# Causal attention without its empty quarter, with a fused score and row extremum

## The reference

```python
s_o = jnp.einsum('bhqd,bhkd->bhqk', qc, ko).astype(jnp.float32) * scale
s_o = s_o + table_h[:, t5_bucket(rel_o)]
s_o = jnp.where(rel_o >= 0, s_o, -jnp.inf)
...
p = jax.nn.softmax(logits, axis=-1)
```

```python
s = jnp.where(mb, s, NEG_INF)
m = jnp.maximum(jnp.max(s, axis=-1, keepdims=True), sink)
p = jnp.exp(s - m)
denom = jnp.sum(p, axis=-1, keepdims=True) + jnp.exp(sink - m)
return jnp.einsum('bkgqs,bskd->bqkgd', (p / denom).astype(vbb.dtype), vbb)
```

## Time and profile before

| | us |
|---|---|
| median of 3 timed runs | 3369.41 (3365.79 to 3370.77) |
| profiled execution, span from first to last instruction | 3367.9 |
| PE busy in it | 3090.6 (92%) |
| DVE busy | 2435.7 (72%) |
| ACT busy | 1680.4 (50%) |
| POOL busy | 134.1 (4%) |
| mean granted TensorE clock | 0.931 of full |

### The profile page before, as it was taken

How to read it: one execution, slowest core, us unless ns; L and a number is a source line. 1 busy time by engine, 2 the same in 40 slices (tenths; PEclk the granted TensorE clock), 3 DMA queues, 4 the chain that set the end, 5 groups by cost and what they waited for, 6 DMA issues and landing times. The chain is left out here.

```text
span 3367.9 us, 58567 instructions
## 1 busy us (share of the span) xinstructions
PE 3090.6 (92%) x23849; PEld 2753.4 (82%) x23849; DVE 2435.7 (72%) x3648; ACT 1680.4 (50%) x2444; POOL 134.1 (4%) x152
## 2 busy tenths in 40 slices
PE   7679999899888899999987999999899998988899
PEld 6577777689887789898976899899689898978798
DVE  6669999778765468787577587785668788674555
ACT  4437777654552354544553445544554545442444
POOL 0010000100102000000000000000000000011000
PEclk8779999999999799999986999999899999998899
DMA  9347999767410267586430386774057687300442
GB/s 383 141 175 295 370 369 366 292 244 307 188 69 4 78 253 307 225 312 262 162 128 1 119 312 262 265 307 193 11 225 306 231 310 272 123 2 3 160 183 83
DMA packets 77517, 698.67 MB, mean 207 GB/s; under 512 B 8432, under 2 KB 12528, under 8 KB 55408
## 3 DMA queue, kind: packets, MB, share of 16 engines
q1 hardware_dynamic: 30928, 525.65, 39.7%
q10 hardware_dynamic: 42912, 157.31, 12.3%
q0 software_dynamic: 3456, 12.58, 1.0%
HBM read 691.31 MB, written 4.19 MB: 207 GB/s over the span
## 5 line engine op out<-in xcount | busy, mean ns | idle before, releaser
L1074 PE MATMUL banks<-u_split,w_split 128*128 128x512 f32 x2816 | 1014.9, 403 | 22.9 <-DVE u_split L1319 21.0
L1143 ACT ACTIVATE w_split<-ring 128x1024 fp32r<-128x1024 f32 x513 | 541.3, 1058 | 672.1 <-PE banks L1075 406.5
L1250 DVE TENSOR_TENSOR w_split<-ring,w_split 128x1024 fp32r<-128x1024 f32 x513 | 625.5, 1222 | 293.3 <-ACT w_split L1143 288.7
L1075 PE MATMUL banks<-u_split,w_split 128*128 128x256 f32 x2816 | 797.3, 283 | 0.0
L1074 PEld LDWEIGHTS banks<-u_split,w_split 128*128 128x128 f32 x2816 | 537.3, 191 | 158.8 <-issue 17.9
L1075 PEld LDWEIGHTS banks<-u_split,w_split 128*128 128x128 f32 x2816 | 539.7, 192 | 0.0
L1066 PE MATMUL banks<-h_split,w_split 128*128 128x256 f32 x1408 | 400.6, 285 | 7.9 <-DVE w_split L1250 7.9
L1067 PE MATMUL banks<-h_split,w_split 128*128 128x256 f32 x1408 | 400.5, 284 | 0.0
L1068 PE MATMUL banks<-h_split,w_split 128*128 128x256 f32 x1408 | 400.4, 284 | 0.0
L520 PE MATMUL banks<-bufs_split,ring_split 128*128 128x256 f32 x1376 | 397.0, 289 | 0.0
L584 DVE CUSTOM_DVE_ANT_0 bufs<-bufs 128x1024 f32<-128x1024 f32 x300 | 357.0, 1224 | 12.7 <-DVE w_split L1250 12.7
(11 more groups left out here) (489 smaller groups left out, 4931.5 us busy)
## 6 DMA issues: line engine op xcount, KB each, us to landing
ring<-stream SPq DMA_DIRECT2D x155, 3072.0 KB, 10.9
bufs<-ada ACTq DMA_DIRECT2D x296, 512.0 KB, 10.4
bufs<-ada POOLq DMA_DIRECT2D x23, 512.0 KB, 6.7
bufs<-ada SPq DMA_DIRECT2D x3, 2048.0 KB, 16.1
ring<-stream SPq DMA_DIRECT2D x2, 2688.0 KB, 10.0
bufs<-c_rows SPq DMA_DIRECT2D x9, 512.0 KB, 4.3
ring<-stream SPq DMA_DIRECT2D x1, 2704.0 KB, 13.1
ring<-stream SPq DMA_DIRECT2D x1, 2176.0 KB, 8.9
```

Of the source, the lines that this page charges most:

```text
L1074: pe.matmul(bank.rearrange("p (a t) -> p a t", a=2), w_high, u_split[:, k, :, :], start=(k == 0), stop=False, skip_group_check=True)
L1075: return pe.matmul(bank[:, 0:SEQ], w_low, u_split[:, k, 0, :], start=False, stop=(k == KC - 1), skip_group_check=True)
L1143: nc.scalar.activation(w_split[:, slot, 0, :], piece(j, b), ACT.Copy).then_inc(high.sem, 1)
L1250: e = nc.vector.tensor_tensor(w_split[:, slot, 1, :], piece(j, b), w_split[:, slot, 0, :].bitcast(F32), ALU.subtract)
```

## The change

The row of a head now holds 384 columns instead of 512: 128 keys for the first query tile, 256 for the second (`CAUSAL = P + SEQ`). Scores, bias, exponentials, scalings, transposes (three) and the second product with v are cut to it.

DVE's scale, add, maximum and negation become one fused instruction per query tile, which forms minus the scaled score (with a bias that is stored 8 times larger) and keeps the row's minimum, starting from minus the sink. ACT then takes the exponential with scale -1.

The sink becomes a column of the row: POOL writes minus the sink at both ends of the buffer, so the exponential of the row and its sum take it along. The two separate exponentials and the addition on DVE are gone.

```diff
+CAUSAL = P + SEQ
...
-                act.activation(rows[h // 4][:, (h % 4) * 512:(h % 4 + 1) * 512], bank(h), ACT.Copy)\
+                act.activation(rows[h // 4][:, (h % 4) * 512:(h % 4 + 1) * 512], bank(h), ACT.Copy, scale=HEAD ** 0.5)\
...
-                    src = bass.AP(core.scratch.tensor, h * 2 * SEQ + (SEQ - 1) - t * P, [[HEADS_A * 2 * SEQ - 1, P], [1, SEQ]])
-                    sync.dma_start(bias[:, h, t, :], src).then_inc(read.sem, read.count(16))
+                    src = bass.AP(core.scratch.tensor, h * 2 * SEQ + (SEQ - 1) - t * P, [[HEADS_A * 2 * SEQ - 1, P], [1, (t + 1) * P]])
+                    sync.dma_start(bias[:, h, t * P:t * P + (t + 1) * P], src).then_inc(read.sem, read.count(16))
...
+    less_sinks = core.small[:, 96:96 + heads]
+    bank = lambda n, h: core.psum[:, 2 * n + h % 2, :]
+    keys = (slice(0, P), slice(P, CAUSAL))
+    with_sink = (slice(0, P + 1), slice(P + 1, CAUSAL + 2)) if sinks is not None else (slice(1, P + 1), slice(P + 1, CAUSAL + 1))
+    inner = (slice(1, P + 1), slice(P + 1, CAUSAL + 1))
...
+                if sinks is not None:
+                    pool.tensor_scalar(less_sinks, sinks, -1.0, None, ALU.mult).then_inc(sinks_negated.sem, sinks_negated.count(1))
+                    pool.wait_ge(sinks_negated.sem, sinks_negated.at(1))
+                    for h in range(heads):
+                        if h >= 2:
+                            pool.wait_ge(exped.sem, exped.at(h - 1))
+                        pool.tensor_copy(s_buf(h)[:, 0:1], less_sinks[:, h:h + 1])
+                        pool.tensor_copy(s_buf(h)[:, CAUSAL + 1:CAUSAL + 2], less_sinks[:, h:h + 1]).then_inc(sink_placed.sem, sink_placed.count(1))
...
-                    last = pe.matmul(bank(0, h)[:, t, :], q(h)[:, t * P:(t + 1) * P], k(h), start=True, stop=True)
+                    last = pe.matmul(bank(0, h)[:, keys[t]], q(h)[:, t * P:(t + 1) * P], k(h)[:, 0:(t + 1) * P], start=True, stop=True)
...
-                for kt in range(2):
-                    for t in range(2):
-                        last = pe.transpose(bank(1, h)[:, kt, t * P:(t + 1) * P], p_buf(h)[:, t, kt * P:(kt + 1) * P], ident)
+                for part in range(3):
+                    last = pe.transpose(bank(1, h)[:, part * P:(part + 1) * P], p_buf(h)[:, 1 + part * P:1 + (part + 1) * P], ident)
...
+                pe.matmul(rows[:, 0:SEQ], v(h, 0), pt_buf(h)[:, 0:SEQ], start=True, stop=False, skip_group_check=True)
+                pe.matmul(rows[:, P:SEQ], v(h, 1), pt_buf(h)[:, SEQ:CAUSAL], start=False, stop=True, skip_group_check=True)\
...
+            if sinks is not None:
+                dve.wait_ge(sinks_negated.sem, sinks_negated.at(1))
...
-                link(dve.scalar_tensor_tensor(s_buf(h), bank(0, h), scale, bias(h), ALU.mult, ALU.add))
-                link(dve.tensor_reduce(stat(h, 0), s_buf(h), AX, ALU.max))
-                if sinks is None:
-                    last = dve.tensor_scalar(stat(h, 1), stat(h, 0), -1.0, None, ALU.mult)
-                else:
-                    last = dve.tensor_scalar(stat(h, 1), stat(h, 0), sinks[:, h:h + 1], -1.0, ALU.max, ALU.mult)
+                if h >= 2:
+                    dve.wait_ge(exped.sem, exped.at(h - 1))
+                for t in range(2):
+                    last = dve.tensor_tensor_reduce(s_buf(h)[:, inner[t]], bank(0, h)[:, keys[t]], bias(h)[:, keys[t]], -scale,
+                                                    3e38 if sinks is None else less_sinks[:, h:h + 1], ALU.add, ALU.min, stat(h, 0)[:, t:t + 1])
...
+                if sinks is not None:
+                    act.wait_ge(sink_placed.sem, sink_placed.at(h + 1))
...
-                    if sinks is not None:
-                        act.activation(stat(h, 3)[:, t:t + 1], sinks[:, h:h + 1], ACT.Exp, bias=stat(h, 1)[:, t:t + 1])
-                    e = act.activation(p_buf(h)[:, t, :], s_buf(h)[:, t, :], ACT.Exp, bias=stat(h, 1)[:, t:t + 1],
-                                       accum_out=stat(h, 2)[:, t:t + 1])
+                    e = act.activation(p_buf(h)[:, with_sink[t]], s_buf(h)[:, with_sink[t]], ACT.Exp, bias=stat(h, 0)[:, t:t + 1], scale=-1.0,
+                                       accum_out=stat(h, 1)[:, t:t + 1])
```

More of the change, by code:

```diff
@@ L282, in const_plan @@
              ("causal", 2 * P), ("zeros", P), ("slide", 2 * RW_HEADS - 2),
-             ("band", 2 * SEQ), ("buckets", 2 * SEQ)]
+             ("band", CAUSAL), ("buckets", 2 * SEQ)]
     place, at = {}, 0
@@ L316, in const_array @@
     put("causal", np.concatenate([i[:, None] < i[None, :], i[:, None] <= i[None, :]], axis=1).astype(np.float32))
-    band = np.zeros((P, 2, SEQ), np.float32)
+    band = []
     for t in range(2):
-        rel = (t * P + i)[:, None] - np.arange(SEQ)[None, :]
-        band[:, t] = np.where((rel >= 0) & (rel < P), 0.0, NEG)
-    put("band", band.reshape(P, -1))
+        rel = (t * P + i)[:, None] - np.arange((t + 1) * P)[None, :]
+        band.append(np.where((rel >= 0) & (rel < P), 0.0, NEG))
+    put("band", np.concatenate(band, axis=1))
     dist = (SEQ - 1) - np.arange(2 * SEQ)
@@ L1637, in attend @@
                     pe.wait_ge(stored.sem, stored.at(h - 1))
[L1638 to L1642, removed]
+                rows = bank(2, h)[HEAD * (h % 2):HEAD * (h % 2) + HEAD, :]
+                pe.matmul(rows[:, 0:SEQ], v(h, 0), pt_buf(h)[:, 0:SEQ], start=True, stop=False, skip_group_check=True)
+                pe.matmul(rows[:, P:SEQ], v(h, 1), pt_buf(h)[:, SEQ:CAUSAL], start=False, stop=True, skip_group_check=True)\
+                    .then_inc(attended.sem, attended.count(1))
             scores(0)
@@ L1670, in softmax_out @@
                 dve.wait_ge(exped.sem, exped.at(h + 1))
-                if sinks is not None:
[L1672 to L1675, removed]
+                link(dve.reciprocal(stat(h, 2), stat(h, 1)))
+                dve.tensor_scalar(p_buf(h)[:, inner[0]], p_buf(h)[:, inner[0]], stat(h, 2)[:, 0:1], None, ALU.mult)
+                dve.tensor_scalar(p_buf(h)[:, inner[1]], p_buf(h)[:, inner[1]], stat(h, 2)[:, 1:2], None, ALU.mult)\
                     .then_inc(normed.sem, normed.count(1))
@@ L1700, in turned_copy @@
                     act.wait_ge(attended.sem, attended.at(h - 1))
-                act.activation(pt_buf(h), bank(1, h), ACT.Copy).then_inc(turned_sb.sem, turned_sb.count(1))
+                act.activation(pt_buf(h), bank(1, h)[:, 0:CAUSAL], ACT.Copy).then_inc(turned_sb.sem, turned_sb.count(1))
             def head_out(h):
@@ L1705, in head_out @@
                 base = HEAD * (h % 2)
-                act.activation(out(h), bank(2, h)[base:base + HEAD, 0, :], ACT.Copy).then_inc(stored.sem, stored.count(1))
+                act.activation(out(h), bank(2, h)[base:base + HEAD, 0:SEQ], ACT.Copy).then_inc(stored.sem, stored.count(1))
             exps(0)
@@ L2344, in first_block @@
     attention_stage(core, HEADS_A, lambda h: rows(qk[:, 0:4, :], h), lambda h: rows(qk[:, 4:8, :], h),
[L2345 to L2348, removed]
+                    lambda h, kt: v_tok[:, kt, HEAD * h:HEAD * h + HEAD], lambda h: bias[:, h, 0:CAUSAL],
+                    lambda h: rows(attn_out, h), lambda h: core.bufs[:, 6, 512 * (h % 2):512 * (h % 2) + CAUSAL + 2],
+                    lambda h: core.bufs[:, 6, 1024 + 512 * (h % 2):1024 + 512 * (h % 2) + CAUSAL + 2],
+                    lambda h: core.bufs[:, 7, 512 * (h % 2):512 * (h % 2) + CAUSAL], beside=lambda pool: later.load(pool, LATER_SUMS["pair_norm"]))
     pair_norm_stage(core, core.buf(0), core.buf(9), (core.col("norm_lru_g"), core.col("norm_attn_g")), later)
@@ L2407, in _ @@
             core.load_ahead(sync, ("sw_v", 0))
-            core.load_const(sync, "band", core.bufs[:, 7, D:D + 2 * SEQ])
+            core.load_const(sync, "band", core.bufs[:, 7, D:D + CAUSAL])
         @block.tensor
@@ L2501, in window_attention @@
     window_projection_stage(core, u, core.mod[:, 3 * KC:4 * KC], qk, v_tok, core.buf(4, 2), lambda c: core.col("q_norm" if c < 8 else "k_norm"))
-    band = core.bufs[:, 7, D:D + 2 * SEQ].rearrange("p (a t) -> p a t", a=2)
+    band = core.bufs[:, 7, D:D + CAUSAL]
     rows = lambda x, c, h: x[HEAD * (h % 2):HEAD * (h % 2) + HEAD, c, :]
```

16 lines of the change are left out of this document (8 added, 8 removed).

## The result

The changed kernel takes 3378.63 us (median of 9 runs, 3373.69 to 3383.89), the kernel before 3370.77 (9 runs, 3365.25 to 3379.30). The ratio is 1.0025, 95% interval 1.0015 to 1.0035: slower by a quarter of a percent where 0.5% faster was forecast. In the one profiled execution of each, the two stages that the change touches took 81.7 us before and take 89.8 now. Over a whole execution the mean granted clock is 0.921 to 0.924 in all nine of the changed kernel, and 0.928 to 0.934 in the 62 fast executions of the kernel before that were timed beside the experiments, so the profiled one is no exception.

What follows compares the result with a forecast made beforehand. PE was taken to bound each head, DVE almost as long; savings of 10.3 us (window stage) and 5.0 (first) sum to 15.3, span 3352.6, plus 1.5 carried over gives 3354, range 3347 to 3362.

Steps and rivals of the forecast that it cites:

- I leave the clock's rise where it was, at 2385.3: Window stage: TensorE's clock still rises to 2.4 GHz at 2385.3; the stage shrinks from 52.6 to 42.3 us.
- rival A: Both attention stages: the clock never rises, the total is 11 us slower at 3380; chance 4%.
- The price of a step: One head's step on PE: 2.12 us at 2.4 GHz, 3.88 at 1.2, with gaps at group boundaries unchanged.
- The fill of the first stage: First attention stage, PE start to first turn (transposes): 6.0 us becomes 4.2.
- That of the window stage: Window stage, PE start to first turn (transposes): 5.4 us becomes 3.4.
- what ACT's new wait holds: Window stage start: POOL's negation and two copies take 1.1 us, against 1.7 until ACT needs them; price 0.
- the 377 ns assumed: Window stage: each one-column POOL copy priced at a similar row's median, 0.75 us per head, hidden.
- Rivals B and C: Attention steps: handovers bind, 3361, chance 8%; or POOL becomes the bound, 3358 to 3359, chance 5%.
- No weight is being loaded while either stage runs: Both attention stages: 0 GB/s of weight loading, cited from the window stretch, so later work shifts as a block.
- shift as a block: Everything after the two stages moves earlier by what they save, 15.3 us in sum.
- rival D: Elsewhere in the program the clock's falls land differently, and 5 us or more go or come; chance 7%.
- PE stays the full engine, exactly as now: Attention stages: argument against the clock never rising, since PE remains the fullest engine; that rival got 4%.

Runs made afterwards that it cites:

- e1: Changed kernel with all of TensorE's columns put back, the surplus unread; 3357.83 us, ratio 0.9969 to the kernel before.
- e7: Kernel before with only the quarter of columns left out; DVE and ACT keep separate instructions, nothing on POOL; 3379.34 us, ratio 1.0036.
- e8: Changed kernel plus only 70 zero products on TensorE in the recurrence stage, ahead of the first attention; 3371.23 us, ratio 1.0019.
- e3: Changed kernel plus zero products in TensorE's pauses: 70 in the recurrence stage, 5 + 5 behind the first scores of each attention stage; 3336.21 us, ratio 0.9905.
- e5: Changed kernel plus only 5 + 5 zero products behind the first scores of each attention stage, none in the recurrence stage; 3348.33 us, ratio 0.9945.
- e9: Changed kernel plus 70 zero products in the recurrence stage and 5 + 1 behind the first scores of each attention stage; 3338.08 us, ratio 0.9915.
- e4: Changed kernel plus one product of a zero tile with 512 columns in each step; 3368.01 us, ratio 0.9987.
- e2: Changed kernel with only the scores' columns put back on TensorE, the extra quarter unread; 3383.93 us, ratio 1.0032.

## Why the prediction was wrong, by its own steps

**The step that failed** is "I leave the clock's rise where it was, at 2385.3", with 139.3 for the first stage. In the changed kernel the rise comes at about 2420 and 154, when the last heads have no scores left. All of the forecast's saving at 2.4 GHz hung on it. The kernel before needed its full columns to bring the clock back: with them it rose in e1, without them (changed kernel, e7, e8) it stayed low. What came is rival A, at 4%: 11 us slower and 3380 were worked out, 8 and 3378.6 measured. Its stages were forecast to lose 2.2 and 8.8 us and lost 0.8 and 7.4.

What held, against the same profile:

- The price of a step: 3.88 at 1.2 GHz (changed kernel) and 2.12 at 2.4 GHz (e3), both to the hundredth. So the gaps at the group boundaries were not shortened by fewer columns, as assumed.
- The fill of the first stage was 4.2 us as worked out. That of the window stage was 2367.88 - 2364.03 = 3.85 and not 3.4. The fused instruction with the sink as start value takes 351 and 480 ns on 128 and 256 columns; without it, in the first stage, 293 and 421. And ACT's table load waits for POOL:

```profile
2364.73 0.18 POOL L1629 COPY bufs<-small 128x1 f32<-128x1 f32 x1
2364.75 1.28 ACT L1704 ACT_TABLE_LOAD   x1 [9.24 <-POOL bufs L1629]
...
2366.05 0.41 ACT L1704 ACTIVATE bufs<-bufs,small 128x129 f32<-128x129 f32 x1
```

Before the change it stood at the very start of the stage (2368.43, where PE starts at 2368.47), under the wait for the scores. Now it ends at 2366.05, after the row extremum (2365.83), 0.2 us late. That is half of what the fill is over the forecast. I had counted what ACT's new wait holds, but not the table load behind it.

- DVE, ACT and POOL are off the path: DVE waits for PE 32 us, ACT 28.8, and the copies took half of the 377 ns assumed. Rivals B and C are refuted by e3, whose steps are 2.12.
- "No weight is being loaded while either stage runs" holds for the window stage only. In the first the loads that POOL starts are under way (249 GB/s in 132 to 137 of e8); no run shows that they cost the stage anything. Nor did all that comes later shift as a block: the profiled span grew by 3.9 us where the stages lost 8.1, since the span from 684 to 1188 us came out 4.3 shorter. That is rival D at work in one execution. The medians, 7.9 apart, have no such gain.

**Why A was given 4%.** "PE stays the full engine, exactly as now" was the argument against it, and it was read from the busy share. The busy share was 100% in 2380 to 2383 in the earlier trace rows, at half clock; the prediction noted it, and concluded only that being busy did not raise the clock at once. It was the warning, and the stretches ahead of it are the same:

```profile
2374.00:2377.00 3.00, 3.00 (x9) 1.83 (x10) 2.18 (x7) 2.30 (x9) 0.00 (x0) 0.50 0.00 0
2377.00:2380.00 3.00, 3.00 (x9) 1.52 (x9) 2.45 (x7) 1.85 (x6) 0.00 (x0) 0.50 0.00 0
```

In this trace a full busy share stood beside a clock that did not rise for 11 us, from 2374 to 2385, so the busy share could not vouch for the clock when a quarter of TensorE's columns was taken out. What the Trainium skill says under "TensorE: Matmul & The Clock Gate", section "A second HAM failure mode: psum-queue depth-cycling", that short pauses between groups of matmuls make the clock fall to half rate again and again, is not what happened either: e3 has the gaps between its groups in every step, 0.52 of 2.12 us by the prediction's working, and stays at 1.00. What happened is that a low clock isn't regained. In the first stage it was low from the start, in the window stage the fill lost it. e8 shows the loss in both, e1 and e5 two ways to regain it.

The range, 3347 to 3362, left A out by its 4%. The rows gave no ground for so small a chance: the kernel before regained it late in both stages, and the change took columns out of just the work that regained it.

## What to carry to other kernels

A step whose matmuls get shorter must be priced at both levels of the clock, and the level asked for by itself: where in the trace did it rise, under which work, and does the change thin out just that work? Where a pipeline's fill leaves TensorE idle for a microsecond or two, a few products of a zero tile there can be worth more than the change to the loop. In this kernel 10 of them in each stage, alone, turned 8 us lost into 18 won (e5), and with a burst in the idle stage before it, 28 (e9).

## What the hardware showed that I had not expected

- The same loop runs at either clock, and in these traces it kept what it had: 3.88 us a step at 1.2 GHz for some 50 us (changed kernel), 2.12 at 2.4 GHz for some 30 (e3).
- Work that nobody needs, put into every step, made the changed kernel faster twice: e1 by 21 us and e4 by 11 (19 and 13 by the ratios).
- The clock does not always come back at the same place: in e2, one kernel, two executions of ten were some 20 us faster than the others, with the higher mean clocks.
- The fused instruction takes some 58 ns more in the window stage, where its start value comes from memory, than in the first, where it is a constant (351 against 293 ns on 128 columns, 480 against 421 on 256). No run changed the start value alone.
